# Expert stage: the down matrices are loaded from ACT's DMA queue, the gate and up matrices stay on SP's

## What is computed

```python
hg = silu(x @ w_gate[e]) * (x @ w_up[e])     # w_gate, w_up: 2048 x 512
hg = hg * gate[:, e]
y = y + hg @ w_down[e]                       # w_down: 512 x 2048
```

## Time and profile before

| | before |
|---|---|
| time, median of 3 runs | 2095.07 us (2093.65 to 2096.19) |
| time of the profiled execution | 2095.07 us |
| span of the profiled execution | 2093.1 us |
| PE busy | 1840.8 us (88%) |
| ACT busy | 400.9 us (19%) |
| DVE busy | 484.6 us (23%) |
| POOL busy | 53.5 us (3%) |
| DMA, mean over the span | 242 GB/s, 505.82 MB |
| mean granted TensorE clock | 0.954 |

### The profile page before, as it was taken

One profiled execution on the slowest core, in us unless ns is written; L12 is line 12 of the kernel. 1 busy time (PEld: TensorE's weight loads), 2 busy tenths in 40 slices (PEclk: granted clock), 3 DMA queues, 4 the chain that ended last, 5 costly groups with the idle time before them and its releaser, 6 DMA issues.

```text
span 2093.1 us, 29565 instructions
## 1 busy us (share of the span) xinstructions
PE 1840.8 (88%) x11998; PEld 1345.0 (64%) x11998; DVE 484.6 (23%) x1116; ACT 400.9 (19%) x1077; POOL 53.5 (3%) x94
## 2 busy tenths in 40 slices
PE   4999999879999999999959988888888998888882
PEld 3788888568889995466647555555645556555451
DVE  1111100677777763010240000000000000000003
ACT  2310000555556551011210000000000000000001
POOL 0000000000000000000000000000000000000000
PEclk9999999979999999999969999999999999999996
DMA  8424653000000007354226999999999999999993
GB/s 286 161 81 161 113 131 141 1 1 1 0 0 0 0 1 274 135 194 161 86 81 256 428 432 418 420 425 434 423 428 420 431 419 425 429 435 428 430 419 159
DMA packets 93162, 505.82 MB, mean 242 GB/s; under 512 B 39076, under 2 KB 43416, under 8 KB 74680
## 3 DMA queue, kind: packets, MB, share of 16 engines
q1 hardware_dynamic: 85456, 487.62, 57.6%
q0 software_dynamic: 6656, 14.12, 1.9%
q10 hardware_dynamic: 1000, 3.37, 0.5%
HBM read 498.76 MB, written 18.91 MB: 247 GB/s over the span
## 4 chain that ended last, share of the span: by engine, by line
PE 69%; DMA 21%; DVE 4%; ACT 3%; issue 2%; SPq 1%; DVEq 0%; ACTq 0%; POOLq 0%
DMA ring<-in_wu 18%; PE ps L1558 16%; PE ps L1211 13%; PE ps L1455 5%; PE ps L1597 5%; PE ps L1548 5%; PE ps L1372 3%; PE ps L1391 3%; PE ps L1473 3%; DMA ring<-in_wd 2%; PE ps L1347 2%; PE ps L1397 1%; PE ps L1514 1%; PE ps L1482 1%; SPq L264 1%
## 5 line engine op out<-in xcount | busy, mean ns | idle before, releaser
L1558 PE MATMUL ps<-ring,rkv 128*64 128x256 f32 x4096 | 484.9, 399 | 73.9 <-DMA ring<-in_wu 42.9
L1558 PEld LDWEIGHTS ps<-ring,rkv 128*64 128x64 f32 x4096 | 335.6, 144 | 232.4 <-DMA ring<-in_wu 51.2
L1211 PE MATMUL ps<-hnT,ring 128*128 128x256 f32 (+1 forms) x1280 | 280.7, 382 | 6.4 <-ACT gg L455 2.2
L1211 PEld LDWEIGHTS ps<-hnT,ring 128*128 128x128 f32 (+1 forms) x1280 | 240.3, 188 | 47.1 <-issue 8.7
L1597 PE MATMUL ps<-ring,gg 128*64 128x512 f32 x1024 | 231.9, 606 | 23.1 <-DMA ring<-in_wd 11.9
L1597 PEld LDWEIGHTS ps<-ring,gg 128*64 128x64 f32 x1024 | 82.3, 139 | 150.6 <-issue 136.6
L1157 DVE SCALAR_TENSOR_TENSOR gg<-ps,tmp,gg 128x256 f32<-128x256 f32 x32 | 15.5, 484 | 532.0 <-PE ps L1558 532.0
L1548 PE MATMUL ps<-hnT,sw 128*128 (+1 forms) x1024 | 120.8, 280 | 7.4 <-DVE hnT L1141 7.4
L1548 PEld LDWEIGHTS ps<-hnT,sw 128*128 128x128 f32 x1024 | 117.8, 195 | 13.3 <-issue 13.3
L1372 PE MATMUL ps<-ring 128*128 128x128 f32 x768 | 114.7, 276 | 0.1
L1372 PEld LDWEIGHTS ps<-ring 128*128 128x128 f32 x768 | 100.3, 192 | 0.8 <-ACT ring L545 0.3
(11 more groups left out here) (315 smaller groups left out, 1719.1 us busy)
## 6 DMA issues: line engine op xcount, KB each, us to landing
ring<-in_wg SPq DMA_DIRECT2D x32, 4096.0 KB, 19.9
ring<-in_wu SPq DMA_DIRECT2D x32, 4096.0 KB, 20.6
ring<-in_wd SPq DMA_DIRECT2D x32, 4096.0 KB, 18.0
ring<-in_w_in SPq DMA_DIRECT2D x7, 4096.0 KB, 14.3
ring<-in_w_out SPq DMA_DIRECT2D x4, 4096.0 KB, 15.8
ring<-in_w_in SPq DMA_DIRECT2D x16, 512.0 KB, 7.5
ring<-in_xatt_wk SPq DMA_DIRECT2D x1, 4096.0 KB, 13.6
ring<-in_xatt_wv SPq DMA_DIRECT2D x1, 4096.0 KB, 13.6
```

The lines of the kernel that those rows point to most:

```text
L1211: ins = mm(ps[0:rows_, t % 4, 0:T], lhs, hnT[:, k, :], start=k == 0, stop=k == KD - 1)
L1558: ins = mm(ps[CAP * h:CAP * h + CAP, bank, 0:T], xT[:, k, CAP * i:CAP * i + CAP], slot_k(slot)[:, k, T * h:T * h + T], start=k == 0, stop= ...
```

## The change

SP issues only the gate and up matrices of the loop over the experts. The down matrices go out from ACT, on ACT's queue: a helper `down_weights(e)` waits for the same count of `m_dn` as SP did and issues the same transfer into the same slot. It is called ahead of `job(e)`, and so behind the copy L641 of the job before. The first down matrix (expert 0) is still issued by SP. `weights` itself is unchanged but for the engine, which it now takes as an argument.

```diff
+        def weights(eng, s, name, e):
...
+            eng.dma_start(dst, src).then_inc(landed[s], 16)
...
             def expert(e, j):
                 sp.wait_ge(S["m_gate"], j + 1)
-                weights(S_GATE, "wg", e)
+                weights(sp, S_GATE, "wg", e)
                 sp.wait_ge(S["m_up"], j + 1)
-                weights(S_UP, "wu", e)
-                sp.wait_ge(S["m_dn"], 2 * j + 1)
-                weights(S_DOWN, "wd", e)
+                weights(sp, S_UP, "wu", e)
...
                 with sp.Fori(1, blocks) as b:
-                    with sp.Fori(0, NE) as e:
+                    expert(0, b * NE)
+                    sp.wait_ge(S["m_dn"], 2 * NE * b + 1)
+                    weights(sp, S_DOWN, "wd", 0)
+                    with sp.Fori(1, NE) as e:
                         expert(e, b * NE + e)
...
+                def down_weights(e):
+                    act.wait_ge(S["m_dn"], 2 * NE * b + 2 * e + 1)
+                    weights(act, S_DOWN, "wd", e)
+
...
                 job(b * NE, first=True)
+                down_weights(1)
                 job(b * NE + 1, then=b * (NE // 2) + 1)
                 with act.Fori(1, NE // 2 - 1) as d:
+                    down_weights(2 * d)
                     job(b * NE + 2 * d)
+                    down_weights(2 * d + 1)
                     job(b * NE + 2 * d + 1, then=b * (NE // 2) + d + 1)
+                down_weights(NE - 2)
                 job(b * NE + (NE - 2))
+                down_weights(NE - 1)
                 job(b * NE + (NE - 1))
```

More of the change, by code:

```diff
@@ L264, in rows @@
                 eng.dma_start(praw[r:r + src.shape[0], i, 0:src.shape[1]], src).then_inc(S[done], 16)
+        def weights(eng, s, name, e):
+            if s == S_DOWN:
+                dst = slot_d(s).rearrange("p (h c) n -> p h (c n)", h=2)
+                src = a[name][ds(e, 1)].rearrange("o (h p c) n -> p (o h) (c n)", h=2, p=P)
+            else:
+                dst = ring[:, s, :]
+                src = a[name][ds(e, 1)].rearrange("o (p k) n -> p (o k n)", p=P)
+            eng.dma_start(dst, src).then_inc(landed[s], 16)
         @block.sync
@@ L290, in _ @@
                     sp.dma_start(dst, src).then_inc(landed[s], 16)
[L292 to L299, removed]
             def expert(e, j):
                 sp.wait_ge(S["m_gate"], j + 1)
-                weights(S_GATE, "wg", e)
+                weights(sp, S_GATE, "wg", e)
                 sp.wait_ge(S["m_up"], j + 1)
-                weights(S_UP, "wu", e)
-                sp.wait_ge(S["m_dn"], 2 * j + 1)
-                weights(S_DOWN, "wd", e)
+                weights(sp, S_UP, "wu", e)
             for s, name in ((S_GATE, "wg"), (S_UP, "wu"), (S_DOWN, "wd")):
                 sp.wait_ge(used[s], static[s])
-                weights(s, name, 0)
+                weights(sp, s, name, 0)
             sp.wait_ge(S["r_cntv"], 1)
```

## The result

| | before | after |
|---|---|---|
| time, median (4 runs each) | 2094.36 us (2092.67 to 2096.19) | 2118.85 us (2114.96 to 2122.11) |
| time of the profiled execution | 2095.07 us | 2118.93 us |
| its span | 2093.1 us | 2116.9 us |
| expert stage, pair of jobs | 59.74 us | 61.57 us |
| DMA share and rate, 1137 to 2047 us | 1.00, 425 GB/s | 0.98, 414 GB/s |

The changed kernel is slower: ratio 1.0116, 95% interval 1.0097 to 1.0135, some 24 us. That is little, but clear of the noise. The forecast was 2121 us.

A forecast was written before the change was run, and what follows sets the result against it. The prediction took DMA throughput to bound the expert stage. Issues counted 0 and a 1.75 us gap in each of 15 pairs added 26 us to 2095.07, giving 2121 us, range 2094 to 2162.

The forecast's parts named there:

- The bound: Expert stage: DMA throughput limits it; time is bytes over rate plus DMA idle time, that second term zero before.
- The issues at 0: SP's and ACT's queues: moving 31 issues of 0.38 us from SP to ACT brings 0, since both have idle time.
- One run in turn, shares of 2/3 and 1/3: DMA engines, both queues busy: each turn serves one run per queue, SP's 32 KB and ACT's 16 KB.
- The walk through a pair: Expert stage, two jobs traced by issue and landing: 61.5 us instead of 59.74, over 15 pairs 26 us more.
- the start of the walk: Plain job's down matrix, issued at time 0: moves alone from 1.15 to 8.2 us, then 8.7 us at 1/3.
- The gap: Expert stage, before the next pair's first down matrix moves: both queues empty for 1.75 us per pair.
- The slow product: Down product that PE has waited for: takes 2.9 us more than 7.1, with 0 and 1.7 as other values.
- no slow products, +71: Upper bound from the walk: down products not slowed after waits make a pair 64.5 us, +71 us in all.
- The bound for equal shares, +67: Upper bound from the walk: queues sharing bytes equally make a pair 64.2 us, +67 us in all.
- Gap closed: Rival for the expert stage: shifted phases keep one queue filled, DMA share stays 1.00, 2095 to 2099 us; chance 0.13.
- Long turns: Rival on DMA engines: many runs of one queue are served before turning, +109 us, 2204 us; chance 0.08.
- faster: Rival on DMA engines: two queues fill small pauses between runs, 27 us less, 2068 us; chance 0.07.

The follow-up runs named there:

- 16 against 16 KB: Changed kernel with gate, up and down matrices all in runs of 16 KB, against the kernel before: 2101.71 us, ratio 1.0037.
- 32 against 32 KB: Changed kernel with the down matrix in one 32 KB run per partition, like gate and up, against the kernel before: 2142.70 us, ratio 1.0227.

## Why the prediction was right

**The bound.** A share of 1.00, hence a stage whose time is bytes over rate plus idle time of the DMA engines: held. The 24 us lost are the fall from 425 to 414 GB/s in that stretch, and no run was faster than the kernel before by more than the noise.

**The issues at 0.** Held: with all 93 transfers issued by ACT the time is that of before.

**One run in turn, shares of 2/3 and 1/3.** Held, as far as the runs can tell. The down matrix above moved 9.9 us worth by these shares where it needs 9.96. Making its runs alone shorter or longer changed the time (2263, 2119 and 2143 us), while halving all runs left it (2120 us). The miss at 16 against 16 KB says that the shares are not all that the time hangs on. The Trainium skill ("DMA: Bandwidth & Descriptors", "Queues, rings and completion order") has an engine drain a whole packet of one queue, typically some 9 to 17 descriptors, before it switches to another. If a run is a descriptor, the trace does not agree: a down matrix would have landed some 12 us after its issue and PE would have waited for the up matrix; it landed after 23, and PE waited for the down matrix.

**The walk through a pair: 61.5 us.** Measured 61.57, and 15 x 1.75 = 26 us stands against 24. The total is right, but not every line of the walk. I had both down matrices waited for, by 2.4 us in the plain job and 1.5 in the select job, landing after 18 and 23. In the trace the plain job waits 4.7 to 10.2 us and its down matrix lands after 23; the select job waits 2.5 us or less. The step that was off is the start of the walk: I let the up matrix before end 1.75 us ahead of the plain job's down matrix, and by the estimate above it moves for 2.6 us more beside it. So that matrix is alone for 4.3 us instead of 7.05, and the rest of it at 1/3 takes 14.1 us instead of 8.7.

The gap lies in another place too. I had it ahead of the plain job's down matrix; it is ahead of the select job's. By the same shares, from the measured issues, the gate matrix of 1542.16 is through at about 1558 and the up matrix of 1548.92 at about 1568, while the down matrix issued at 1567.84 begins at 1569.0: a gap of 1 us, where the profile has the share of 0.51.

The slow product took 9.1 us, 2.0 more than 7.1 (8.4 to 10.0 in the other plain jobs), and only in the plain job, where I took 2.9 in both jobs. And the idle gap is smaller than 1.75 us, about 1.1 (1.8% of 61.57). The pair is 1.83 us longer than before, so some 0.7 to 0.8 us are the lower rate while both queues move, for which I had no term. So that 2121 came so near to 2118.85 is partly luck: these errors met. The bound "no slow products, +71" fell too: without PE's long waits and at a clock of 0.99 the kernel was 5 us faster, not slower. The bound for equal shares, +67, was too high as well: 16 against 16 KB cost 7 us and 32 against 32 KB 48.

**A sentence to correct.** I wrote that PE needs the down matrix last. Of an expert's three that is so; of the three that are under way together it is the one that PE needs first, since gate and up belong to the next expert. That is why it hurts when the others take part of its rate; the walk had the order right.

**The rivals.** *Gap closed*: it did not. The Trainium skill ("DMA: Bandwidth & Descriptors", "Issuing engines are not separate DMA queues") has the transfers of all issuing engines run on the same 16 DMA engines and interleave. The trace agrees, in that the rate did not rise with the second queue (425 GB/s before, 414 after). But interleaving is not neutral when transfers are needed in an order. *Long turns* and *faster*: no sign of either.

## What to carry to other kernels

When the DMA engines are busy all the time and the transfers already stand in one queue in the order in which they are needed, a second queue has nothing to bring, and it lets later transfers take rate from earlier ones; here that cost 24 us with the down matrix moved and 26 us with the up matrix. If two queues must be used at once, look at the length of the contiguous runs on each: in these runs it set their shares, and with the wrong ratio the same bytes took some 150 us more. A change of queue can be judged ahead by one walk through the loop with the shares. Here such a walk gave the sign of the loss and, partly by luck, its size; it did not give the place where the loss shows.

## What the runs showed that I had not expected

- The run length acts like a priority between queues. Down matrices in runs of 8, 16 and 32 KB beside 32 KB runs gave 2263, 2119 and 2143 us (the last may be a long pattern), on one queue 2101, 2095 and 2094. The scatter's landings move too: median 11.8 us before, 9.5 with down matrices in 8 KB runs and 15.0 in 32 KB runs on one queue; on two queues 14.9 in the changed kernel, 19.0 with 32 KB on both and 8.6 with 8 KB on both. That fits rows that wait for a run of each other queue that moves just then; it was not tested by itself.
- At equal shares one kernel had two times, 50 us apart (2113 and 2166 us), without any change of input or code.
- Keeping PE at its full clock through its waits (0.99 instead of 0.93 in the stage) gave 5 us of the 24: in a loop that waits for transfers a slow product costs little.
